# Entry of the mixer's input projection in one block with its preparation, bonus products on GpSimd

## The reference

```python
mod = jax.nn.silu(c) @ ada_w[l] + ada_b[l]
u = modulate(rmsnorm(x, norm_mix_g[l]), sh_mix, sc_mix)
p = u @ w_in[l]                       # 1024 -> 2816 columns
y_conv = conformer_conv(p[..., :2 * CONV_CH], ...)          # uses a * sigmoid(b)
xs = token_shift(p_rwkv, mu)          # p + mu * (prev - p)
r, k, v, wl, al, gl = jnp.split(xs, RWKV_SPLITS, axis=-1)
w = -jax.nn.softplus(-(w0 + jnp.tanh(wl) @ w2)) - 0.5
a = jax.nn.sigmoid(a0 + al @ a2)
g = jax.nn.sigmoid(gl) @ g2
kk = k * k_k
k = k * (1 + (a - 1) * k_a)
...                                   # the recurrence over time gives y
bonus = jnp.sum(r_h * k_h * r_k, axis=-1, keepdims=True) * v_h
y = y * gn_w + gn_b + bonus
return y * g
```

## Time and profile before

| what | value |
|---|---|
| median of three runs | 1360.62 us (1360.62 to 1361.96) |
| the profiled execution's own time | 1359.24 us |
| its span | 1357.3 us |
| PE busy | 1189.9 us (88%) |
| DVE busy | 955.0 us (70%) |
| ACT busy | 433.7 us (32%) |
| POOL busy | 273.5 us (20%) |
| first matmul of the input projection | starts at 37.75 us |
| last instruction of the input projection | ends at 119.78 us |

### The profile page before, as it was taken

How to read it: one execution, slowest core, us unless ns; L and a number is a source line. 1 busy time by engine, 2 the same in 40 slices (tenths; PEclk the granted TensorE clock), 3 DMA queues, 4 the chain that set the end, 5 groups by cost and what they waited for, 6 DMA issues and landing times. The chain is left out here.

```text
span 1357.3 us, 19952 instructions
## 1 busy us (share of the span) xinstructions
PE 1189.9 (88%) x7724; PEld 814.2 (60%) x7724; DVE 955.0 (70%) x2122; ACT 433.7 (32%) x919; POOL 273.5 (20%) x264
## 2 busy tenths in 40 slices
PE   4898998989888888878888777788999989999998
PEld 1787866745343433324233222235999979999998
DVE  0595336699786877868787786577778989666552
ACT  2652225421111111101101001015676484544431
POOL 0000000044444443444444344430000000000000
PEclk9899998989999999999999999999999999999999
DMA  9456159899999999999999999996485715566553
GB/s 390 172 203 219 24 207 426 338 409 392 422 421 421 421 421 421 419 421 417 420 416 408 421 414 406 420 417 277 156 340 210 289 63 187 208 242 242 184 215 120
DMA packets 50766, 428.18 MB, mean 315 GB/s; under 512 B 5744, under 2 KB 7920, under 8 KB 8304
## 3 DMA queue, kind: packets, MB, share of 16 engines
q0 software_dynamic: 36864, 268.45, 47.9%
q1 hardware_dynamic: 13808, 158.46, 30.3%
HBM read 423.51 MB, written 1.05 MB: 313 GB/s over the span
## 5 line engine op out<-in xcount | busy, mean ns | idle before, releaser
L1524 PE MATMUL bank<-arena 128*128 128x512 f32 x1024 | 501.1, 619 | 108.9 <-DVE arena L1717 108.6
L1524 PEld LDWEIGHTS bank<-arena 128*128 128x128 f32 x1024 | 178.4, 191 | 414.4 <-DVE arena L1717 273.9
L1791 DVE CUSTOM_DVE_ANT_0 arena<-arena 128x1024 f32<-128x1024 f32 x256 | 313.2, 1223 | 135.3 <-DMA arena<-experts_in,arena 134.1
L1413 POOL DMA_INDIRECT arena<-experts_in,arena x256 | 272.9, 1066 | 604.4 <-PE bank L1524 355.4
L560 PE MATMUL bank<-rounded,rounded 128*128 128x256 f32 x1264 | 371.3, 294 | 21.2 <-DVE rounded L511 12.0
L561 PE MATMUL bank<-rounded,rounded 128*128 128x256 f32 x1264 | 360.0, 285 | 0.0
L562 PE MATMUL bank<-rounded,ring_r 128*128 128x256 f32 x1264 | 359.7, 285 | 0.0
L560 PEld LDWEIGHTS bank<-rounded,rounded 128*128 128x128 f32 x1264 | 244.4, 193 | 30.1 <-issue 14.3
L529 DVE TENSOR_TENSOR ring_r<-ring,rounded 128x1024 fp32r<-128x1024 f32 (+2 forms) x155 | 194.5, 1262 | 96.5 <-ACT rounded L524 95.6
L561 PEld LDWEIGHTS bank<-rounded,rounded 128*128 128x128 f32 x1264 | 244.4, 193 | 4.2 <-issue 3.9
L562 PEld LDWEIGHTS bank<-rounded,ring_r 128*128 128x128 f32 x1264 | 244.2, 193 | 0.0
(11 more groups left out here) (286 smaller groups left out, 984.3 us busy)
## 6 DMA issues: line engine op xcount, KB each, us to landing
ring<-slots_in SPq DMA_DIRECT2D x68, 2048.0 KB, 8.5
arena<-slots_in SPq DMA_DIRECT2D x4, 2048.0 KB, 23.6
arena<-experts_in,arena POOLq DMA_INDIRECT x256, 13.6
xT<-xT_in SPq DMA_DIRECT2D x1, 1024.0 KB, 11.1
mixT<-slots_in SPq DMA_DIRECT2D x1, 1024.0 KB, 29.4
out_dram<-xT SPq DMA_DIRECT2D x1, 1024.0 KB, 3.9
arena<-slots_in SPq DMA_DIRECT2D x1, 768.0 KB, 9.2
uT<-arena SPq DMA_DIRECT2D x4, 142.0 KB, 9.7
```

The lines of the kernel that those rows point to most:

```text
L1413: pool.indirect_dma_start(rows[:, r % GRING, :], None, experts_in, bass.IndirectOffsetOnAxis(ap=expert[:, tt, at:at + 1], axis=0)).then_in ...
L1524: ins = pe.matmul(psum[2 * tt + half][:, :], diag[:, r % DIAGS, :], rows[:, r % GRING, D + 512 * half:D + 512 * half + 512], start=(h == 0 ...
L1791: dve.tensor_tensor_reduce(rows[:, r % GRING, 0:D], rows[:, r % GRING, 0:D], utok[:, tt, :], 1.0, 0.0, ALU.mult, ALU.add, hdot[:, r:r + 1] ...
```

## The change

The preparation and the input projection become one block, so that the engines no longer meet between them. The constants are loaded in two parts: 256 columns (`ident` and `ones`, 128 KB) where the whole stood, the rest (424 KB) behind slot 4, with a semaphore `rest_ready` for those who read it. Tiles 0 and 1 are made by `plain_pieces`; `Split` has the 20 tiles 2 to 21, so `dve_lo(j)` belongs to tile j + 2. PE runs `keep_busy` between parts of the modulation and ahead of the plain pieces. LoRA products come after tile 3, the decay's sigmoids after the copy of tile 3. The bonus products go to POOL, which starts when DVE raises `rk` and raises it again at the end. Gate and bonus products and `fgsq` go into the recurrence, one or two instructions behind certain evictions.

```diff
-                pe.wait_ge(nm_sq, KT * norms[0] + k + 1)
+                pe.wait_ge(nm_sq, k + 1)
...
-        win = Split([(WIN[i // 4], 512, (i % 4) * P, i) for i in range(NTILE)], KT, uT, KEPT, in_mm, buffers=4)
+        win = Split([(WIN[i // 4], 512, (i % 4) * P, i) for i in range(PLAIN, NTILE)], KT, uT, KEPT, in_mm, buffers=4)
+        FIRST = 2 * P
...
-                load_slots(sp, after("ada"), after("w_in_b"))
+                sp.dma_start(vec[:], vecs_in).then_inc(vec_ready, 16)
+                load_slots(sp, 0, 1)
+                sp.dma_start(con[:, 0:FIRST], consts_in[:, 0:FIRST]).then_inc(con_ready, 16)
+                sp.dma_start(xT[:], xT_in).then_inc(x_ready, 16)
+                load_slots(sp, 1, after("ada", 1))
+                sp.dma_start(con[:, FIRST:], consts_in[:, FIRST:]).then_inc(rest_ready, 16)
+                load_slots(sp, after("ada", 1), after("w_in_b"))
...
+                pool.wait_ge(vec_ready, 16)
+                pool.wait_ge(rw["rk"], 1)
+                for ct in range(CT):
+                    pool.tensor_scalar(T2[:, ct, :], xs[:, ct, :], vcol("rwkv_r_k", ct), None, ALU.mult).then_inc(seq_g, 1)
+                pool.wait_ge(seq_g, CT)
+                pool.tensor_tensor(T2, T2, T0, ALU.mult).then_inc(rw["rk"], 1)
...
+                pe.wait_ge(c_ready, 2)
+                pe_mod(pe, 0, 0, 2)
+                pe.wait_ge(con_ready, 16)
+                pe_sum_squares(pe)
+                pe_mod(pe, 0, 2, 4)
+                keep_busy(pe, 2)
+                pe_mod(pe, 0, 4, 6)
+                keep_busy(pe, 4)
+                pe_mod(pe, 0, 6, KT)
+                pe_mod_cols(pe, 0)
+                keep_busy(pe, 4)
+                plain_pieces(pe, WIN[0], in_mm)
...
-                for i in range(NTILE):
+                for i in range(PLAIN, NTILE):
...
-                    if i == 4:
+                    if i == 3:
                         lora_products()
...
-                        pe.wait_ge(rw["rk"], 1)
+                        pe.wait_ge(rw["rk"], 2)
                         pe.wait_ge(rw["gout"], 2)
                         head_sums(3, T2, rw["bonus"])
...
                 for i in range(GLU_AT):
-                    win.act_hi(act, i + LEAD)
+                    if i >= PLAIN and i != 4:
+                        win.act_hi(act, i - PLAIN + LEAD)
                     act.wait_ge(in_mm, i + 1)
...
-                    elif i == 5:
+                    elif i == 3:
+                        win.act_hi(act, 4 - PLAIN + LEAD)
                         for ct in range(CT):
...
                 mix_norm.dve(dve, win)
                 dve.wait_ge(in_zero, 4)
+                shift(12, 14, 2)
                 win.dve_lo(dve, 3)
                 win.dve_lo(dve, 4)
-                shift(12, 14, 2)
+                shift(4, 6, 4)
                 win.dve_lo(dve, 5)
-                win.dve_lo(dve, 6)
                 dve.wait_ge(rw["sigw"], CT)
+                dve.wait_ge(rest_ready, 16)
...
-                win.dve_lo(dve, 12)
-                for ct in range(CT):
-                    v(dve.tensor_scalar(T2[:, ct, :], r[:, ct, :], vcol("rwkv_r_k", ct), None, ALU.mult))
-                dve.tensor_tensor(T2, T2, T0, ALU.mult).then_inc(rw["rk"], 1)
-                win.dve_lo(dve, 13)
+                win.dve_lo(dve, 10)
+                dve.sem_inc(rw["rk"], 1)
+                win.dve_lo(dve, 11)
...
-                dve.wait_ge(rw["rk"], 1)
+                dve.wait_ge(rw["rk"], 2)
                 v(dve.tensor_tensor(T0, T0, T3, ALU.mult))
...
+        GATE_AT = (("L3R", 0), ("L3R", 1), ("G1", 2), ("L1R", 2))
...
+                def bonus_and_gate(k, c):
+
+                    if k in ("L1R", "L2R") and c < 2:
+                        ct = 2 * (k == "L2R") + c
+                        v(dve.scalar_tensor_tensor(bv[:, ct, :], bv[:, ct, :], vcol("rwkv_gn_b", ct), gate[:, ct, :],
+                                                   ALU.add, ALU.mult))
+                    elif (k, c) in GATE_AT:
+                        ct = GATE_AT.index((k, c))
+                        v(dve.tensor_scalar(gate[:, ct, :], gate[:, ct, :], vcol("rwkv_gn_w", ct), None, ALU.mult))
+                    elif (k, c) == ("L3R", 2):
...
+                    bonus_and_gate(k, c)
```

More of the change, by code:

```diff
@@ L400, in build @@
         mix_norm = Norm(gain[:, 0, :], mod1[:, 0:8])
[L401 to L446, removed]
         pB = area(0, NPROJ, T + 1)
@@ L648, in _ @@
                     elif i == 8:
+                        pe.wait_ge(rest_ready, 16)
                         pe.wait_ge(rw["sq"], 1)
@@ L658, in _ @@
             def _(act):
+                act.wait_ge(vec_ready, 16)
+                act.wait_ge(c_zero, 1)
+                act.activation(csil[:, 0, :, 0], vcol("c", 0, 8), ACT.Silu).then_inc(c_ready, 1)
+                act.activation(csil[:, 1, :, 0], vcol("c_2", 0, 8), ACT.Silu).then_inc(c_ready, 1)
+                act.wait_ge(eps_ready, 4)
+                act.preload_act_table_set("natural_log_exp_and_others")
+                act.wait_ge(x_ready, 16)
+                act_squares(act, lambda k: None)
+                mix_norm.act_rstd(act)
+                act_mod(act, 0)
                 mix_norm.act(act, win, rooted=True)
                 for i in range(GLU_AT):
-                    win.act_hi(act, i + LEAD)
+                    if i >= PLAIN and i != 4:
+                        win.act_hi(act, i - PLAIN + LEAD)
                     act.wait_ge(in_mm, i + 1)
@@ L709, in _ @@
                 v = chain("v", dve, seq_v)
+                dve.memset(csil[:], 0.0).then_inc(c_zero, 1)
+                for j, e in enumerate((RMS_EPS, LN_EPS, GN_EPS, 1.0)):
+                    dve.memset(epsc[:, j:j + 1], e).then_inc(eps_ready, 1)
+                dve.wait_ge(vec_ready, 16)
+                v(dve_mod(dve, 0))
+                v(dve.scalar_tensor_tensor(gain[:, 0, :], mod1[:, 8:16], 1.0, vcol("norm_mix_g", 0, 8), ALU.add, ALU.mult))
+                dve.wait_ge(x_ready, 16)
                 r, k = xs[:, 0:4, :], xs[:, 4:8, :]
@@ L734, in _ @@
                                            ALU.add).then_inc(rw["L"], 1)
-                win.dve_lo(dve, 7)
-                shift(4, 6, 4)
-                win.dve_lo(dve, 8)
+                win.dve_lo(dve, 6)
                 shift(6, 8, 6)
@@ L741, in _ @@
                 dve.tensor_tensor(bv, T4, T4, ALU.mult).then_inc(rw["sq"], 1)
-                win.dve_lo(dve, 9)
+                win.dve_lo(dve, 7)
                 dve.wait_ge(rw["a"], CT)
@@ L747, in _ @@
                 v(dve.scalar_tensor_tensor(T0, T0, 1.0, k, ALU.add, ALU.mult))
-                win.dve_lo(dve, 10)
+                win.dve_lo(dve, 8)
                 shift(0, 2, 8)
-                win.dve_lo(dve, 11)
+                win.dve_lo(dve, 9)
                 for h in range(2):
@@ L782, in _ @@
                                         xs[:, 8 + 2 * h:10 + 2 * h, :], ALU.mult))
+                win.dve_lo(dve, 17)
+                win.dve_lo(dve, 18)
                 win.dve_lo(dve, 19)
-                win.dve_lo(dve, 20)
-                for ct in range(CT):
-                    v(dve.scalar_tensor_tensor(bv[:, ct, :], bv[:, ct, :], vcol("rwkv_gn_b", ct), gate[:, ct, :],
-                                               ALU.add, ALU.mult))
-                for ct in range(CT):
-                    v(dve.tensor_scalar(gate[:, ct, :], gate[:, ct, :], vcol("rwkv_gn_w", ct), None, ALU.mult))
-                v(dve.tensor_scalar(fgsq[:, 0:4], vcol("final_g", 0, 4), 1.0 / D, None, ALU.mult))
-                v(dve.tensor_tensor(fgsq[:, 0:4], fgsq[:, 0:4], vcol("final_g", 0, 4), ALU.mult))
-                v(dve.tensor_scalar(fgsq[:, 4:8], vcol("final_g", 4, 4), D ** -0.5, None, ALU.mult))
-                win.dve_lo(dve, 21)
                 dve.wait_ge(in_ev, GLU_AT)
@@ L1063, in statistics @@
                                           ALU.mult).then_inc(rc_y, 1)
+                def bonus_and_gate(k, c):
[7 more added lines that the diff above has]
+                    elif (k, c) == ("L3R", 2):
+                        v(dve.tensor_scalar(fgsq[:, 0:4], vcol("final_g", 0, 4), 1.0 / D, None, ALU.mult))
+                        v(dve.tensor_tensor(fgsq[:, 0:4], fgsq[:, 0:4], vcol("final_g", 0, 4), ALU.mult))
+                        v(dve.tensor_scalar(fgsq[:, 4:8], vcol("final_g", 4, 4), D ** -0.5, None, ALU.mult))
                 for k, c in ORDER:
```

16 lines of the change are left out of this document (8 added, 8 removed).

## The result

The changed kernel takes 1346.21 us (median of 4 runs, 1345.73 to 1348.83), the kernel before in the same comparison 1361.15 us. The ratio is 0.9894, 95% interval [0.9877, 0.9911]: 1.1% faster. 1346.3 was predicted. The agreement to 0.1 us is luck: the profiled execution was predicted at 1344.9, and the distance from it to the median was taken as 1.4 us, as before, and is 0.3 now. The profiled execution took 1345.87 us, its span is 1343.7.

A forecast was written before the change was run, and what follows sets the result against it. The projection was taken as bound by PE up to 63.9 us, then by DVE's list; the recurrence by PE. -15.3 + 0.7 + 0.3 = -14.3 us gave 1344.9 for the profiled execution, median 1346.3, range 1343.5 to 1349.

The forecast's parts named there:

- Entry: Block start: slots 1 to 4 come 1.0 us earlier; plain tiles start at 33.3 and are through at 40.1.
- Rival A: At the entry: PE's granted clock is down, half speed costs 2.8 us, 1349.1; chance 0.2 together with Rival B.
- Sigmoids and scan: Projection: the decay's last sigmoid is done at 50.1, so the scan starts at 50.2, 12.4 us earlier.
- DVE's list: DVE's work from the scan to the first L799: 43.2 us plus 1.3 us of waits, ending at 94.7.
- My first paragraph: Profile reading: the projection is bound by PE up to 63.9 us, then by DVE's late and overfull list.
- my walk: Both engines' projection lists followed against each other: PE 9 us behind DVE, last product at 104.5, 15.3 us less.
- PE's list: PE's projection work from 47.9 us to 103.9, making PE the bound instead of DVE.
- POOL: Bonus products on POOL take 4 us, bounds 3.4 and 5.3; 11.7 us are there before PE needs them.
- The term of 0.7: Projection: loss from POOL working beside DVE, taken as 0.7 us within 0 to 3.1.
- Rival B: Projection: DVE loses what POOL takes, 5.3 us less slack of 2.2, 1348.7; chance 0.2 together with Rival A.
- Recurrence and stalls: Recurrence: 4.24 us of moved DVE work costs 0.3 us; changed PE stalls, between -2.7 and +2.7, taken as 0.
- the 0.3 I took: Recurrence: cost of the moved DVE pieces, at most 4.2 us if their cover were gone.

The follow-up runs named there:

- gate products back: The changed kernel with gate and bonus products and fgsq put back into the projection, behind dve_lo(18); ratio 0.9920 to the kernel before.

## Why the prediction was right

*Entry.* The first plain matmul at 33.3 was predicted and stands at 33.30; the plain tiles done at 40.1, tile 2 starts at 40.09. The clock held, and the traces with and without `keep_busy` put this term at 2.9 us. Rival A is out for the profiled execution, but it is near: in the kernel with POOL's scalings twice, slot 4 was a microsecond late and the clock fell.

*Sigmoids and scan.* 50.2 predicted, 50.74 measured. I had the decay's last sigmoid as what comes last. In the trace it was DVE's own list: the sigmoid was done at 50.40, and the scan followed a subtraction, since the one at 46.69 had waited 2.09 us for ACT's cast, which stood behind tanh.

*DVE's list.* 43.2 us of work and 1.3 of waits were predicted; the last `dve_lo` ended at 98.3 instead of 94.7. The first L788, for which 94.7 stood, began at 98.19. These 3.5 us are the scan's 0.5, POOL's 2.6 and 0.3 of waits (0.88 and 0.74 where I had 1.3 in all). My first paragraph said that DVE starts its list too late and has too much on it. The runs bear out only the first: with the 6.9 us back on it the projection is 0.3 us longer, which is in line with the 9 us that DVE was ahead in my walk.

*PE's list.* 103.9 predicted, 105.1 measured for the end of the last tile. The bound did change to PE. What was missing is 0.5 us before the tile at 90.65 and about 0.7 spread over the rest.

*POOL.* Here the size was off. I took 4 us with bounds of 3.4 and 5.3; it took 11.7. The bounds came from a memset and a gather, and neither reads 256 elements with a scalar for each partition. The rule that I quoted from the Trainium skill (SBUF — State Buffer, "Who interferes with whom") fits the traces: DVE's instruction of two SBUF inputs that started beside POOL's wide product took 2.62 us instead of 0.41. It ended 0.27 us behind POOL's. The other figure from the Trainium skill (GPSIMD Engine Reference, "Elementwise — side-by-side cycle accounting"), 4497 ns for 2048 elements, gave as an estimate 2.25 us for the wide product, measured 2.68 beside a busy DVE, and as much for the four small ones, where 8.95 was measured. That my sum came out is partly luck: 11.7 us just fitted into the 11.7 that I had worked out between POOL's start and DVE's need of the result (in the trace DVE wanted it at 86.3, 3.5 us after POOL's end), and DVE's loss was then nearly what it had to spare. The term of 0.7 that I took is near the 0.6 that the run with the bonus products on DVE shows, but it was a guess within 0 to 3.1. Rival B was nearer to what happened: DVE lost 2.6 us and had 2.2 to spare, which left 0.5 for PE. Only its size was off, for DVE didn't lose what POOL took: of POOL's 11.7 us, 8.95 went by while DVE's instructions of 128x1024 took 1.22 to 1.30 us each.

*Recurrence and stalls.* No cost of the moved pieces can be seen: DVE's busy time there rose from 20.5 to 24.3 us and PE's from 57.1 to 58.6, and the stage behind the projection kept its length within 0.5 us. It scatters by 6.6 us over fourteen traces, so the 0.3 I took can't be seen in it: the eight with the pieces in the recurrence average 1236.0 us, the six without 1237.3.

So -15.3 + 0.7 + 0.3 stood for what the trace has as -14.1 in the projection and +0.5 behind it, -13.6 in all. The sum is right to 0.7 us, and the mechanism behind its large term, an earlier scan and then PE as the bound, is what the runs show.

## What to carry to other kernels

When an engine's list is late, look first for the wait ahead of the list (8.97 us here) and only then at what stands on it: starting it earlier, with one shift put ahead of it, brought 8.1 us; taking 6.9 us of work off it was worth 0.3 once it started early, and nothing where it started late. Work handed to POOL was not off DVE's list here: DVE gave away 2.68 us and lost 2.6 in the changed kernel and 2.85 in the kernel before. And filling PE's gaps ahead of a burst was worth 2.9 us of the projection for matmuls that nobody reads; in these traces no gap of up to 0.99 us at that place was followed by a lower clock, and of the longer ones some were.

## What the runs showed that was not expected

- Four POOL products of 128x256 with a scalar for each partition took 8.95 us beside a busy DVE, and 6.03 us where DVE stood idle for part of the time; the same scaling as one product of 128x1024 with a broadcast operand took 2.79 us.
- A gap of 0.99 us on PE left the granted clock at 1.00. Of three longer gaps at the same place, those of 2.81 and 2.39 us were followed by 0.50, and one of 2.51 us (gate products back) was not; the length of the gap alone doesn't decide it. A stand of 3.04 us at the second head sums, behind uninterrupted work, was followed by 0.57 and 0.50.
- Slot 4's arrival, behind some 9 MB of loads, differed by 1.8 us (31.33 and 33.15) between runs of kernels that issue the same DMAs, and the first cast, placed ahead of the first shift, passes each of these microseconds on.
